# Matmuls with unread results ahead of TensorE's first waits, and a weight unit split ahead of the first tokens, in a one-core two-block model kernel

## What is computed

```python
def first_block(x, norm_mix, ...):
    for layer in range(DEPTH):
        h = rms_norm(x, norm_mix[layer])          # layer 0: the opening of the kernel
        if layer % N_MIXERS == 0:
            y = stick_breaking_attention(h, sb_w_qkv[ia], sb_w_o[ia])
    ...

def stick_breaking_attention(h, w_qkv, w_o):
    qkv = (h @ w_qkv).reshape(B, S, 3, SB_HEADS, SB_HEAD_DIM)
    ...
```

## Time and profile before

| | |
|---|---|
| median of 3 runs | 1521.88 us (1521.64, 1521.88, 1522.43) |
| profiled execution, its own time | 1521.64 us |
| its span, first to last instruction | 1519.6 us |
| PE busy in the span | 1324.5 us (87%) |
| DVE, ACT, POOL busy | 1066.6, 544.9, 533.2 us (70%, 36%, 35%) |
| chain that ended last, by engine | PE 55%, POOL 28%, issue 10%, DVE 4%, DMA 1%, ACT 1% |

### The profile page before, as it was taken

The page is one execution under the profiler, slowest core; times in us unless marked ns, Lnnn a source line. Parts: engine busy times, 40 slices in busy tenths (PEclk is TensorE's granted clock), DMA queues, the critical chain, the costliest instruction groups (busy, mean ns, idle before and its releaser), DMA issues.

```text
span 1519.6 us, 22076 instructions
## 1 busy us (share of the span) xinstructions
PE 1324.5 (87%) x8142; PEld 955.3 (63%) x8142; DVE 1066.6 (70%) x2105; ACT 544.9 (36%) x1037; POOL 533.2 (35%) x620
## 2 busy tenths in 40 slices
PE   8999999999999999999999999677777776666665
PEld 7998998889899888888888874222222222222221
DVE  5566775569877556897777798974857577776655
ACT  6665654458666454432244232120303030201010
POOL 8300001000000000000000477777777777777772
PEclk9999999999999999999999999799999998999998
DMA  8444656544665555231139699999999999999996
GB/s 255 153 149 139 186 192 208 193 139 139 194 189 190 197 188 165 84 113 59 58 121 320 225 413 412 411 415 415 416 416 416 416 415 417 416 416 416 415 416 265
DMA packets 184158, 408.93 MB, mean 269 GB/s; under 512 B 10690, under 2 KB 91884, under 8 KB 184060
## 3 DMA queue, kind: packets, MB, share of 16 engines
q0 software_dynamic: 74096, 269.52, 44.0%
q1 hardware_dynamic: 109660, 137.06, 28.0%
q10 hardware_dynamic: 304, 1.05, 0.2%
HBM read 406.54 MB, written 1.05 MB: 268 GB/s over the span
## 4 chain that ended last, share of the span: by engine, by line
PE 55%; POOL 28%; issue 10%; DVE 4%; DMA 1%; ACT 1%; DVEq 0%; POOLq 0%; ACTq 0%
PE banks L2468 13%; PE banks L2469 12%; PE banks L2470 12%; POOL arena L943 12%; POOL wring L943 9%; POOL h_raw L943 4%; PE banks L2956 4%; PE banks L2705 3%; PE banks L2714 3%; POOL sq L943 2%; PE banks L2811 1%; DMA wring<-in_expert_v_dram,eidx 1%; PE banks L2417 1%; PE banks L2722 1%; PE banks L2935 1%
## 5 line engine op out<-in xcount | busy, mean ns | idle before, releaser
L943 POOL DMA_INDIRECT arena<-in_expert_u_dram,eidx x115 | 109.4, 951 | 649.1 <-DVEq L2212 614.3
L1458 DVE TENSOR_TENSOR w_a_low<-wring,w_a_high 128x1024 fp32r<-128x1024 f32 x192 | 234.9, 1227 | 116.9 <-ACT w_a_high L982 114.0
L982 ACT ACTIVATE w_a_high<-wring 128x1024 fp32r<-128x1024 f32 x192 | 200.9, 1051 | 106.7 <-PE banks L2470 106.2
L2468 PE MATMUL banks<-h_high,w_a_high 128*128 128x256 f32 (+1 forms) x832 | 237.8, 286 | 0.9 <-DVE h_low L1480 0.7
L2997 PE MATMUL banks<-arena 128*128 128x512 f32 x360 | 183.3, 641 | 60.8 <-DMA arena<-in_expert_v_dram,eidx 59.1
L2469 PE MATMUL banks<-h_low,w_a_high 128*128 128x256 f32 (+1 forms) x832 | 235.1, 283 | 0.0
L2470 PE MATMUL banks<-h_high,w_a_low 128*128 128x256 f32 (+1 forms) x832 | 233.5, 281 | 0.0
L2997 PE MATMUL banks<-wring,arena 128*128 128x512 f32 x280 | 141.5, 636 | 60.6 <-DMA wring<-in_expert_v_dram,eidx 56.1
L2997 PEld LDWEIGHTS banks<-arena 128*128 128x128 f32 x360 | 66.5, 201 | 177.3 <-issue 159.9
L2267 DVE CUSTOM_DVE_ANT_0 arena<-arena,banks 128x1024 f32<-128x1024 f32 x101 | 122.8, 1217 | 63.4 <-DMA arena<-in_expert_u_dram,eidx 62.8
L2468 PEld LDWEIGHTS banks<-h_high,w_a_high 128*128 128x128 f32 x832 | 156.2, 188 | 2.9 <-issue 1.4
(11 more groups left out here) (449 smaller groups left out, 2463.0 us busy)
## 6 DMA issues: line engine op xcount, KB each, us to landing
wring<-in_mlp_w_dram SPq DMA_DIRECT2D x64, 1024.0 KB, 5.3
wring<-in_w_in_dram SPq DMA_DIRECT2D x19, 1024.0 KB, 5.2
wring<-in_sb_w_qkv_dram SPq DMA_DIRECT2D x11, 1024.0 KB, 7.3
wring<-in_rg_w_in_dram SPq DMA_DIRECT2D x8, 1024.0 KB, 5.3
wring<-in_sb_w_o_dram SPq DMA_DIRECT2D x4, 1024.0 KB, 5.1
wring<-in_rg_w_o_dram SPq DMA_DIRECT2D x4, 1024.0 KB, 5.0
wring<-in_w_o_dram SPq DMA_DIRECT2D x4, 1024.0 KB, 6.7
arena<-in_w_q_dram SPq DMA_DIRECT2D x4, 1024.0 KB, 9.1
```

The lines of the kernel that those rows point to most:

```text
L943: g.indirect_dma_start(out=grow(j), out_offset=None, in_=(expert_u, expert_v)[which][0], in_offset=bass.IndirectOffsetOnAxis(ap=eidx[:, tt ...
L982: a.activation(unit(n, 0), raw_unit(n), ACT.Copy).then_inc(w_high, 1)
L1458: v.tensor_tensor(unit(n, 1), raw_unit(n), unit(n, 0).bitcast(F32), ALU.subtract).then_inc(w_split, 1)
L2468: mm(dst, left[0], right[0], start=first, stop=False)
```

## The change

Four places are edited. On ACT, the high part of weight unit 0 is made ahead of the first tokens instead of behind the first four tiles, and that of unit 1 behind the first four tiles instead of behind all eight. On DVE the low parts of these units move in the same way. On PE, `keep_busy(n)` issues n matmuls of `ident` by `ident` (128 x 128, float32) into bank 7, whose result nobody reads: one ahead of the wait for the gain's row, five ahead of the wait for the first half of x, two ahead of the wait for the second half.

```diff
@@ ACT @@
+            split_high()
             act.wait_ge(g0_ready, 1)
             for j in range(KT // 2):
                 pb = wait_group(act, f"T0_{j}")
                 for kt in (2 * j, 2 * j + 1):
                     a.activation(h_hl[0][:, kt, real], pb[:, t_cols(kt)], ACT.Copy,
                                  scale=g0[:, kt:kt + 1]).then_inc(h_high, 1)
-                if j % 2:
+                if j == 1:
                     split_high()
@@ DVE @@
             dve.sem_inc(g0_ready, 1)
+            split_low()
             for j in range(KT // 2):
                 low(0, j)
-                if j % 2:
+                if j == 1:
                     split_low()
             split_low(2)
@@ PE @@
+            def keep_busy(count):
+
+                for _ in range(count):
+                    mm(bank[BANKS - 1][:, 0:P], ident[:], ident[:], start=True, stop=True)
+
             pe.wait_ge(consts_built, 1)
+            keep_busy(1)
             pe.wait_ge(g0_loaded, 16)
             pb = open_bank("g0")
             transposed(pb[:, 0:KT], rows[0:KT, 0, :], KT).then_inc(group_done, 1)
             for j in range(KT // 2):
                 pb = open_bank(f"T0_{j}")
                 if j % 2 == 0:
+                    keep_busy(2 if j else 5)
                     pe.wait_ge(x_loaded[j // 2], 16)
```

## The result

The changed kernel takes 1523.86 us (median; 1522.78 to 1525.95 in 22 runs) beside 1521.92 (1521.04 to 1524.61 in 22 runs) of the kernel before: ratio 1.0012, 95% interval [1.0007, 1.0018]. It is 1.9 us slower, where 0.7 us less was forecast. The profiled execution took 1522.93 us, its span is 1521.0.

The account below looks back on a forecast made before the run. The opening's chain up to PE's first products and the spread was taken to bound the kernel. Both aims were worth 2.3 us at PE, 1.6 going into the wait for `dgr`: 1521.88 - 0.7 = 1521.2 us, range 1520.0 to 1522.8.

Parts of the forecast that it names:

- Part 2: Opening, PE: the added matmuls fit into idle time at no price; fast products would bring PE to the spread 2.3 us sooner.
- a gain in the opening reaches the end whole: Whole kernel: PE's later waits and the gathers move with the opening, so its gain arrives whole and no stage multiplies it.
- Part 1: Opening, ACT and DVE: weight unit 0 ahead of the tokens moves the first product from 11.06 to about 10.0; ACT 0.34 later.
- Part 3: End of opening: PE waits for `dgr` at 17.86, the spread starts at 17.9 instead of 18.63, gain 0.7 us.
- something that I don't see, behind 600 us: Rival, behind 600 us: an unseen effect of either sign; 5 in 100.
- nothing comes of it: Rival: later transfers put `dgr` at 18.5, or a later wait fixed in time takes the gain back; 1521.9 us, 18 in 100.
- Rule against row: PE's new wait at the spread, up to 1.6 us: by an earlier 2.0 us wait it costs nothing, though the skill says idling throttles.
- slower, by the clock: Rival, opening: PE at 1.2 GHz behind the gap, or for all 48 products; 1523.0 or 1523.4 us, 10 in 100.
- Behind 18 us: After the opening: PE's waits hang on work PE itself released, so they move along; everything comes 0.7 us sooner.
- slot 4: Weight transfer landing at 27.82: ACT, 0.7 sooner, waits some 0.5 us for it; covered by slack, no price.

Follow-up runs that it names:

- e7: Changed kernel with ACT's split of weight unit 3 moved from ahead of Ln and Exp to behind the two diagonals: 1524.07 us, 1.0008 of the kernel before.
- e2: Kernel before with only the eight added matmuls, weight splits where they were: 1523.95 us, 1.0012 of the kernel before.
- e1: Changed kernel without `keep_busy` and its calls, so only the new places of the weight splits: 1521.49 us, 0.9998 of the kernel before.
- e8: e7 with e5's later weight load and 385 fulfilled waits on PE: 1524.34 us, 1.0017 of the kernel before.
- e10: e1 with e7's edit, no instruction added on PE: 1521.36 us, 0.9993 of the kernel before.
- e14: Changed kernel with 225 fulfilled waits on PE, 256 added instructions in all: 1522.09 us, 0.9997 of the kernel before.
- e11: e10 with two unread 128x512 matmuls in PE's wait for `m_low`: 1521.62 us, 0.9995 of the kernel before.
- e9: e7 with two unread 128x512 matmuls in PE's wait for `m_low`: 1524.65 us, 1.0017 of the kernel before.
- e5: Changed kernel with one 1 MB weight load, which ran at 672.6 to 676.4 us, released by a later group: 1523.74 us, 1.0008 of the kernel before.
- e6: e1 with 416 fulfilled waits on PE behind 128x512 products: 1523.07 us, 1.0006 of the kernel before.
- e4: Kernel before with 96 fulfilled waits on PE behind groups of three 128x512 products: 1529.2 us, 1.0049 of the kernel before.

## Why the prediction was wrong

Two steps failed: Part 2, which put the price of the added matmuls at nothing, and the claim at the start that a gain in the opening reaches the end whole.

- **Part 1** was right. ACT's first unit was forecast at 6.96 and measured at 6.75, the second at 9.81 (9.64) with a wait of 0.36 (0.38), the sum of squares at 12.34 (12.04), the first product at about 10.0 (9.61). Both landings came about 0.2 us sooner, so ACT was late by 0.04, not 0.34.
- **Part 3** was right: `dgr` is late next, the spread at 17.62 beside 17.9, the gain 1.03 beside 0.7, at its upper bound. The landings are the difference. e7 shows that ACT's list alone held it.
- **Part 2 failed.** It priced the added matmuls by the idle time that covers them and ended in "I take nothing". They cost nothing in the opening (e2 is 1.3 us ahead until 677), and the 31 instructions that they put into PE's list cost 2.6 us at 677 to 707: the gain of 1.0 us became a loss of 1.6. I had looked at where instructions stand in order; "nothing on PE changes its order" was true and missed that the order's *places* change. Of the rivals only "something that I don't see, behind 600 us" (5 in 100) holds this. The first view to ask was there: PE's 0.51 us "<-issue" at 697.03 in the kernel before, in a stretch of 25 ns matmuls, beside a queue of the kind "instruction".
- **"A gain in the opening should therefore reach the end whole"** failed too. It rested on the waits of PE between 18 and 600 us; the stretch that takes the gain lies behind them. Without any added matmul, e1's 0.83 us shrink to 0.29 by the first gather, so by its rows the split alone is worth 0.3 us and not 0.7 (its median, 1521.49 beside 1522.21, and its ratio, 0.9998, do not tell the two apart). The rival "nothing comes of it" named a later wait that takes the gain back; it looked for it at a load.
- **Rule against row.** I took from the earlier trace rows that 2.0 us of idle time do not lower the clock. In the changed kernel that held (granted 1.00 at 376 to 382), in e7, e8, e10 and e14 not, behind the same wait of 1.98 us: four of the thirteen kernels that have it. The Trainium skill, "TensorE: Matmul & The Clock Gate", section "Part 1: The HAM clock gate", says that idling brings the throttle back and that the moment differs from run to run. The traces agree with both: a granted clock of 0.50 in e10 and 1.00 in e11, which filled the wait, and 0.50 in e14 beside 1.00 in the changed kernel, with the same wait. One row was one sample. The gap ahead of the spread (up to 1.31 us) did not drop it in any trace here: granted 1.00 from 17.5 to 22 us in all.
- **The rival "slower, by the clock"** was wrong: the products were 0.12 us apart from the second on and the granted clock was 1.00 behind the gap. That its 1523.0 to 1523.4 lie near the measured 1523.86 is luck.
- **Behind 18 us:** the waits of PE in between moved along as forecast, and slot 4 cost nothing.

## What to carry to other kernels

Every instruction added to an engine moves all the code behind it. Before unread matmuls (or anything else) go in, look for stretches where the engine runs hundreds of very short instructions, and for idle time "<-issue" in them. There the fetch of code can be within tenths of being the bound: 8 instructions cost 2.0 us here, 31 some 2.6 to 3.1, and 96 cost 6.5, of which some 1.8 were the clock's. Look for the packet 2 to 3 us before the wait's end, since not every such gap is a fetch: the kernel before has one of 0.81 us at 330.21 with no packet of q8 between 310.8 and 331.7. To learn whether a loss is of this kind, add fulfilled waits where the engine has cover, until the sum is a multiple of 256 instructions: if the loss goes, it was the place. A wait of PE that costs nothing in one profile can cost the clock in the next, so read it in several profiles. And read the waits of the whole chain, not of its first part, before a gain is carried to the end.

## What the runs showed of the hardware

- PE's code arrives in packets of 16 KB (60 packets, 0.98 MB), 256 instructions each; a waiting PE went on 2.2 to 2.9 us after a packet's start (once 3.2, at e14's small wait), and packets followed each other no closer than 3.3 us (e9; 3.4 in the changed kernel). The Trainium skill, "Runtime: NRT & Kernel Launch", section "Instruction fetch mechanics", states blocks of 16 KiB with 256 instructions. The traces agree. The same section of the Trainium skill calls the cost of crossing a block's bound mostly hidden. At 676 to 707 us it was not: 2.6 us were lost.
- A 1 MB load that has the DMA engines (103.9% at 674 to 676.2) keeps the fetch back: its packet started at 676.37 behind it, at 673.66 with the load moved (e5).
- Fulfilled waits on PE between 128x512 products cost next to no time: with 416 of them (e6) the lead fell by 0.1 us up to 641 us.
- The granted clock fell to 0.50 for some 3 us, 0.5 to 1 us after a wait of 1.98 us had ended, with PE busy, in e7, e8, e10 and e14 and not in the nine others that have the wait. It also fell behind a wait of 2.47 us (e9) and during one of 3.60 (e4), and not behind the 1.79 of the changed kernel.
